# A decoder step's joint into its second network: three units share the wait for the input's low halves, and a table load of the square root moves behind a weight conversion

## What is computed

```
for i in range(2):
    x = x + 0.5 * swiglu(rmsnorm(x, ffn1_norm[i]), ffn1_wi[i], ffn1_wo[i])
    h = rmsnorm(x, mix_norm[i])
    x = x + (mamba2_mixer(h) if i == 0 else window_attention(q(h), K, V) @ w_o)
    x = x + 0.5 * swiglu(rmsnorm(x, ffn2_norm[i]), ffn2_wi[i], ffn2_wo[i])
    gate = sigmoid(rmsnorm(x, ple_norm[i]) @ ple_gate[i])
    x = x + gate * (p[i] @ ple_proj[i])
    if i == 0:
        K, V = shared_kv(rmsnorm(x, kv_norm) @ w_kv)   # k: norm per head, rotary
```

## Time and profile before

| what | value |
|---|---|
| median of three runs | 1195.03 us |
| the profiled execution's own time | 1194.88 us |
| its span | 1193.1 us |
| TensorE busy | 1182.4 us (99%), 9785 matmuls |
| VectorE busy | 866.7 us (73%) |
| ScalarE busy | 700.7 us (59%) |
| GpSimd busy | 243.8 us (20%) |
| granted TensorE clock | 9 tenths or more in all of 40 slices |
| read from and written to memory | 226.87 MB and 13.39 MB |

### The profile page before, as it was taken

The page is one execution under the profiler, slowest core; times in us unless marked ns, Lnnn a source line. Parts: engine busy times, 40 slices in busy tenths (PEclk is TensorE's granted clock), DMA queues, the critical chain, the costliest instruction groups (busy, mean ns, idle before and its releaser), DMA issues.

```text
span 1193.1 us, 26529 instructions
## 1 busy us (share of the span) xinstructions
PE 1182.4 (99%) x9785; PEld 1155.3 (97%) x9785; DVE 866.7 (73%) x1377; ACT 700.7 (59%) x1149; POOL 243.8 (20%) x352
## 2 busy tenths in 40 slices
PE   9999999999999999999999999999999999999998
PEld 8999999998989899999999999999999899999998
DVE  7767646999899768766745987788468867676447
ACT  6455435777786657555546765555369765444345
POOL 1000002412222202122344333231027310000001
PEclk9999999999999999999999999999999999999999
DMA  8755554755445365866786577647743346555552
GB/s 301 245 201 186 180 176 141 262 190 191 151 148 180 118 224 185 331 213 247 280 299 231 211 268 284 224 165 233 252 157 109 100 164 212 179 184 183 176 179 87
DMA packets 63297, 239.90 MB, mean 201 GB/s; under 512 B 7672, under 2 KB 9632, under 8 KB 58848
## 3 DMA queue, kind: packets, MB, share of 16 engines
q1 hardware_dynamic: 56880, 197.83, 47.5%
q0 software_dynamic: 6064, 40.66, 9.4%
q10 hardware_dynamic: 288, 0.54, 0.2%
HBM read 226.87 MB, written 13.39 MB: 201 GB/s over the span
## 4 chain that ended last, share of the span: by engine, by line
PE 84%; DVE 7%; issue 5%; ACT 4%; DMA 0%; DVEq 0%; SPq 0%; POOL 0%; ACTq 0%
PE bank L504 26%; PE bank L505 26%; PE bank L506 26%; ACT whi L1078 2%; DVE wlo L1554 1%; DVE gu L1613 1%; DVE gu L1601 1%; PE bank L870 1%; PE bank L865 1%; PE bank L892 1%; ACT under L1471 1%; DMA raw<-weights 0%; PE bank L922 0%; DVE xl L1702 0%; DVE xl L1573 0%
## 5 line engine op out<-in xcount | busy, mean ns | idle before, releaser
L1554 DVE TENSOR_TENSOR wlo<-raw,whi 128x1024 fp32r<-128x1024 f32 x367 | 456.8, 1248 | 238.1 <-ACT whi L1078 236.9
L504 PE MATMUL bank<-xh,whi 128*128 128x264 f32 x2008 | 576.1, 287 | 1.8 <-issue 0.6
L505 PE MATMUL bank<-xl,whi 128*128 128x264 f32 x2008 | 569.2, 283 | 0.0
L506 PE MATMUL bank<-xh,wlo 128*128 128x264 f32 x2008 | 568.8, 283 | 0.0
L1078 ACT ACTIVATE whi<-raw 128x1024 fp32r<-128x1024 f32 x367 | 385.7, 1055 | 244.9 <-PE bank L506 235.8
L504 PEld LDWEIGHTS bank<-xh,whi 128*128 128x128 f32 x2008 | 378.2, 188 | 5.6 <-issue 2.2
L505 PEld LDWEIGHTS bank<-xl,whi 128*128 128x128 f32 x2008 | 378.4, 188 | 0.9
L506 PEld LDWEIGHTS bank<-xh,wlo 128*128 128x128 f32 x2008 | 376.6, 188 | 0.0
L504 PE MATMUL bank<-hh,whi 128*128 (+1 forms) x896 | 255.6, 285 | 1.1 <-DVE xact L1601 1.0
L506 PE MATMUL bank<-hh,wlo 128*128 (+1 forms) x896 | 255.0, 285 | 0.0
L505 PE MATMUL bank<-hl,whi 128*128 (+1 forms) x896 | 254.4, 284 | 0.0
(11 more groups left out here) (333 smaller groups left out, 1013.2 us busy)
## 6 DMA issues: line engine op xcount, KB each, us to landing
raw<-weights SPq DMA_DIRECT2D x367, 512.0 KB, 3.6
under<-ssm POOLq DMA_DIRECT2D x8, 1024.0 KB, 7.8
xact<-ssm POOLq DMA_DIRECT2D x8, 1024.0 KB, 6.9
out_ssm_s<-xact POOLq DMA_DIRECT2D x8, 1024.0 KB, 5.7
xact<-dtx_rows POOLq DMA_DIRECT2D x5, 1024.0 KB, 10.2
zs<-dtx_rows POOLq DMA_DIRECT2D x2, 1024.0 KB, 13.6
x<-xT SPq DMA_DIRECT2D x4, 264.0 KB, 5.7
xact<-stat_rows POOLq DMA_DIRECT2D x2, 528.0 KB, 6.6
```

What stands on the lines that cost most here:

```text
L504: pe.matmul(out, whi[:, w, c], rh, start=start, stop=False)
L505: pe.matmul(out, whi[:, w, c], rl, start=False, stop=False)
L506: return pe.matmul(out, wlo[:, w, c], rh, start=False, stop=stop)
L1554: dve.tensor_tensor(wlo[:, s, :], raw[:, s, :], whi[:, s, :].bitcast(F32), ALU.subtract).then_inc(lo_ready, 1)
```

## The change

Four places. (1) `unit_pair` on TensorE: in `f1i1` a third unit joins the first two. Behind their products with xh stand those of unit 2, then `sums`, then the products with xl of all three. (2) ScalarE's conversion of that unit moves from behind the last split to ahead of the sigmoid of tile 6. (3) VectorE's conversion of it moves from behind the eight `low_x` to ahead of them. (4) In `kv` ScalarE's table load moves from behind the second square to behind the third conversion. No instruction of an engine's arithmetic is added or removed.

```
@@ TensorE, unit_pair, in the branch for f1i1, behind the high products of units 0 and 1
+                    banks_.append((A0[stage] + 2) % 4)
+                    pe.wait_ge(lo_ready, u + 3)
+                    pe.wait_ge(a_free, A0[stage] + 3)
+                    for k in range(KT):
+                        for w in (whi, wlo):
+                            pe.matmul(bank[banks_[2]][:, 0:N], w[:, (u + 2) % RING, tile(k)], rh[:, k, :], start=k == 0 and w is whi, stop=False)
+                    sums(stage)
                     for k in range(KT):
                         pe.wait_ge(xl_ready, XREADY[stage] + k + 1)
-                        for j in range(2):
+                        for j in range(3):
                             mm = pe.matmul(bank[banks_[j]][:, 0:N], whi[:, (u + j) % RING, tile(k)], rl[:, k, :], start=False, stop=k == KT - 1)
-                    mm.then_inc(unit_used, 2)
+                    mm.then_inc(unit_used, 3)
@@ TensorE, first_units
                 unit_pair(stage, b_wait, stage != "f1i1", rh, rl)
-                if stage == "f1i1":
-                    sums(stage)
-                for j in (2, 3):
+                for j in (3,) if stage == "f1i1" else (2, 3):
                     unit_a(stage, 0, j, b_wait, rh=rh, rl=rl)
@@ ScalarE, gates
                         if j < 6 or gain is None:
                             ahead(gate, 0, j)
+                        elif j == 6:
+                            ahead(gate, 0, 6)
...
                 if gain is not None:
-                    for j in (6, 7):
-                        ahead(gate, 0, j)
+                    ahead(gate, 0, 7)
@@ ScalarE, kv
-                if j == 1:
+                if j == 2:
                     act.preload_act_table(ACT.Sqrt)
```

## The result

The changed kernel takes **1196.53 us** (median of 22 runs, beside 1194.82 for the kernel before in as many): the ratio is 1.0014, with a 95% interval of 1.0008 to 1.0020. So it is 1.7 us slower, where 1.3 faster was forecast, and 1.0 us above the range's upper end. The profiled execution's span is 1194.5 us, against 1193.1. One of the 22 runs, 1635.7 us at a mean granted clock of 0.655, is not in the ratio, and a run at 0.997, where most have 0.999 or 1.0, is 2 to 3 us above its kernel's median wherever such single runs occur here, so the clock is given where it matters.

The account below looks back on a forecast made before the run. TensorE was taken to bound the kernel, only its stops paying. Nothing kept of f1i1's 1.0 us lead plus 1.3 from the table load came off the 1195.03 median, giving 1193.7 us; range 1192.5 to 1195.5.

Parts of the forecast that it names:

- What bounds the kernel: Whole kernel: TensorE, busy in 99% of the span and 84% of the chain; a change pays only where it stops.
- Unit 2's high half earlier: Start of f1i1: ScalarE's 1.0 us conversion fits its 1.36 us idle before tile 6's sigmoid; costed at nothing.
- unit 2's low half ahead of the eight low halves: Start of f1i1: VectorE's 1.2 us conversion begins at 679.95 and, beside GpSimd's additions, ends 0.5 later, at 681.7.
- TensorE through the joint: f1i1's first units: unit 2's high products from 681.7, unit 4 counts from 690.35 against 691.36: 1.0 us lead.
- The table load: kv: converting before the load removes TensorE's stop at f1o1's third bank; 1.3 us won, bounds 1.1 and 1.3.
- the root: Rival, f1o1's bank 5: TensorE waits there nearly as long; only 0.3 off, 1194.7; chance 0.10.
- Kept of the lead: 0: f1i1: if the loop keeps its times, none of TensorE's 1.0 us survives; bounds all of it and less than nothing.
- TensorE's touch at unit 40: f1i1: conversion done at 795.65, first matmul restarts; TensorE catches up with the loop once, its lead nil there.
- the lower bound: f1i1: less than none of the 1.0 us kept if late pieces hit VectorE worse; one more hit costs 0.6.
- The pieces hit worse: slower: Rival, f1i1: earlier late pieces strike VectorE, three more hits of 0.6; 1.8 lost, 1.3 won, 1195.5; chance 0.10.
- five or six hits: f1i1: the number of hits needed for a time over 1197.4, slower beyond measurement's 0.2%; chance 0.04.
- The lead lives: Rival, f1i1: late pieces couple the loop to TensorE, so 1.0 + 1.3 = 2.3 off, 1192.7; chance 0.17.

Follow-up runs that it names:

- e2: Changed kernel with the table load back behind the second square, leaving the three-unit start of f1i1 alone: 1197.35 us, ratio 1.0022.
- e5: Kernel before, with GpSimd's 24 late pieces of f1i1 (state update) an eighth as wide, waits, signals and transfers kept: 1193.81 us, ratio 0.9993.
- e3: Changed kernel with 11 spare matmuls (1.33 us of TensorE) between f1i1's units 3 and 4: 1193.83 us, ratio 0.9992.
- e6: Changed kernel with GpSimd's 24 late pieces of f1i1 an eighth as wide, waits, signals and transfers kept: 1192.51 us, ratio 0.9979.
- e7: Changed kernel, nothing left out, with the 24 late pieces released by VectorE's takes instead of TensorE's ending a unit: 1192.93 us, ratio 0.9983.
- e9: Changed kernel with only the first 8 of the 24 late pieces (units 4 to 15) an eighth as wide: 1192.80 us, ratio 0.9985.
- e4: Changed kernel with 6 spare matmuls (0.73 us of TensorE) between f1i1's units 3 and 4: 1193.96 us, ratio 0.9997.
- e1: Kernel before with only the table load in kv moved: 1193.69 us, ratio 0.9992.
- e11: Changed kernel, nothing left out, 24 late pieces released by VectorE's takes of the unit after (5, 7, 9, ... 43, mostly odd): 1206.80 us, ratio 1.0100.
- e8: Kernel before with the table load moved and the 24 late pieces released by VectorE's takes: 1193.76 us, ratio 0.9991.

## Why the prediction was wrong, point by point

- **What bounds the kernel** was right: TensorE, and only its stops pay.
- **Unit 2's high half earlier, unit 2's low half ahead of the eight low halves, TensorE through the joint**: right to 0.1 us in every term. The additions of squares cost the conversion 0.55, not 0.5.
- **The table load**: the stop of 1.3 us went, as forecast, and the root wasn't next. By the runs the move is worth 1.2 alone and 0.8 beside the joint, where the stop that it takes away was shorter (e2). So it is not a quantity of its own: with the loop on time (e5) there is no stop left to take away.
- **"Kept of the lead: 0"** is the step that failed. It measured -3.2: 0.9 was won and 4.1 lost. The reasoning was "if the loop keeps its times", and the loop didn't. Three things in it were wrong. First, I read TensorE's touch at unit 40 as the only place where slack matters and never worked out how much cushion the loop has when the pieces begin; the earlier trace rows and the count of unit 4 gave it: 1.2 us, nearly the lead itself. What TensorE gains in time, the loop that feeds it loses in cushion. Second, I priced the lower bound with one hit of 0.6, as though a hit stood for itself. The runs show 1.6 and 0.3 us for two groups of pieces apart and 4.0 for them together: the loop has a cushion that absorbs hits until it is used up. Third, I put at nothing what the pieces release in their turn: GpSimd's transfers of 1 MB come before unit 11's weights now, ScalarE waits 1.90 us for these, and the cushion falls from 2.3 at unit 10 to nothing at unit 12. e3's profiled run had the 1.2 us of cushion at unit 4 back, and that alone did not save it.
- **The rival "The pieces hit worse: slower"** named half of the mechanism, the hits, with a chance of 0.10, and its price was too small: 1.8 lost until unit 40 against 3.2 measured over the key sums. With 3.2 in the place of 1.8 it gives 1195.03 - 1.3 + 3.2 = 1196.9, and 1196.7 by the 1194.82 of these runs, against 1196.53 measured. The range ended at this rival's own forecast, with nothing above it for its size, and it was the unbounded one: nothing in the trace capped the number of hits, and 24 pieces lay on the way. (Its "five or six hits" for 1197.4 were counted short as well: 1197.4 - 1193.7 is 3.7 us, over six hits of 0.6.)
- **"The lead lives"**: e6 (1192.51), e7 (1192.93) and e9 (1192.80) are where it lives, as forecast for it at 1192.7, once the first eight pieces don't come in its way. That its condition, pieces tied to TensorE, is what kills it was the wrong way round.
- By the Trainium skill (SBUF — State Buffer, Who interferes with whom) a VectorE instruction with two SBUF inputs and one of GpSimd that reads SBUF shut each other out, and one with a single SBUF input isn't held up. The traces agree: VectorE's takes, one input of which is in PSUM, have a mean of 424 and 423 ns in the stretch where products have 823 (first fences of "Which pieces").

What stays open: how many of the 4.1 us go to the late transfer and how many to the hits, since no run changes the order of the transfers and leaves the pieces; and what differs between two executions of e3 or e4 that take different courses. Both profiled ones took the slower and have the late transfer, so its order is the first thing to look at; no trace of a faster one was taken.

## What to carry to other kernels

Before an engine on the critical path is made earlier, work out the cushion of what feeds it at that point (end of the feeding conversion to start of use), and whether work on a third engine, and the transfers that this one issues, are timed by it: if the cushion is about as large as the lead, and shared resources are hit in between, the lead can be lost several times over. Such side work belongs on the clock of the engine that it disturbs, in a pause of that engine, not on the clock of the one that it doesn't touch (e7, 3.6 us for a change of one wait and a table). And read the rows of waits that are new, small ones too: one wait of 1.90 us stood in the view above, below totals of 18 to 52. And when a gain fails to come, delaying the favoured engine a little (e3) is a cheap test of whether phase is the cause; look at the single runs and not at the median alone.

## What the runs showed of the hardware that was not expected

- Two courses of one and the same program, 3.5 us apart: in e4 six executions at 1192.2 to 1194.0 and five at 1196.4 to 1197.3. What chooses between them no trace here names; the profiled slower ones of e3 and e4 have a late weight transfer (next point).
- The transfer of unit 11's weights (512 KB) took 9.3 to 10.3 us in seven traces in which it was issued behind the first of two GpSimd transfers of 1 MB each, and 7.7, 5.9 and 4.0 us in the kernel before, e1 and e5, where it was issued ahead of them.
- A switch of a release by one take, on the same work, moved the kernel by 14 us (e7 to e11), of which 6 are one wait for a transfer out of a tile that is used again.
- In e11 TensorE stood still for 6.1 us (824.1 to 830.3); its granted clock was 0.50 (1.2 GHz) from about 828.6 to 835.4 us. In e8's profiled execution, with a mean of 0.997, it was 0.50 from 944 to 950 us, behind short stops from 932 to 942; e7 has the like stops there and no such stretch, and what parts the two no trace shows.
- A table load of 1.28 us, with the conversion 0.01 behind it (822.39 after 821.10 + 1.28), costs nothing where ScalarE would have waited for a slot (e5: 0.23 us of wait left behind the load).
